# The samples' cross-attention in a decoder step: DRAM round trips and a two-slot ring against column tiles and a four-slot ring

## What is computed

```python
def _cross_attend(h, mk, mv, w_cq, w_co):
    b, t, _ = h.shape
    q = (h @ w_cq).reshape(b, t, CROSS_HEADS, CROSS_HEAD_DIM) * CROSS_HEAD_DIM ** -0.5
    s = jnp.einsum('bthe,bmhe->bhtm', q, mk).astype(jnp.float32)
    p = jax.nn.softmax(s, axis=-1).astype(mv.dtype)
    o = jnp.einsum('bhtm,bmhe->bthe', p, mv).reshape(b, t, D_MODEL)
    return o @ w_co
```

## Time and profile before

| | |
|---|---|
| median of 3 runs | 4460.27 us |
| profiled execution, its span | 4467.6 us |
| TensorE busy (matmuls) | 3948.9 us, 88% |
| VectorE busy | 1918.9 us, 43% |
| ScalarE busy | 1238.4 us, 28% |
| prompt's cross-attention, first score matmul to last copy | 2447.97 to 2518.2 us |
| samples' cross-attention, first VectorE instruction to the first of "co" on ScalarE | 2518.71 to 2682.23 us |

### The profile page before, as it was taken

The page is one execution under the profiler, slowest core; times in us unless marked ns, Lnnn a source line. Parts: engine busy times, 40 slices in busy tenths (PEclk is TensorE's granted clock), DMA queues, the critical chain, the costliest instruction groups (busy, mean ns, idle before and its releaser), DMA issues. The chain is left out here.

```text
span 4467.6 us, 73766 instructions
## 1 busy us (share of the span) xinstructions
PE 3948.9 (88%) x30029; PEld 3593.7 (80%) x30029; DVE 1918.9 (43%) x2612; ACT 1238.4 (28%) x1462; POOL 77.4 (2%) x120
## 2 busy tenths in 40 slices
PE   8989986757629998888998879999999999999998
PEld 8989975532228886778998419999999999999997
DVE  3224347758685555433232113333434334343343
ACT  3111126647613333422131202221211212122122
POOL 0000000000000000000000000000000000000000
PEclk9999988879858888999999989999999999999999
DMA  4322237759500000472222352222222222222222
GB/s 151 114 104 85 94 131 245 246 186 375 198 38 1 0 0 15 158 259 99 84 76 103 113 191 94 75 86 95 86 95 95 86 95 86 95 90 91 93 88 77
DMA packets 104474, 501.85 MB, mean 112 GB/s; under 512 B 14305, under 2 KB 20898, under 8 KB 67650
## 3 DMA queue, kind: packets, MB, share of 16 engines
q1 hardware_dynamic: 98082, 479.16, 30.1%
q0 software_dynamic: 6208, 19.93, 1.2%
HBM read 474.55 MB, written 24.50 MB: 112 GB/s over the span
## 5 line engine op out<-in xcount | busy, mean ns | idle before, releaser
L2112 PE MATMUL ps<-hf_hi,whi_f 128*128 128x260 f32 x2816 | 568.3, 283 | 19.1 <-DVE x L2102 11.1
L2112 PE MATMUL ps<-hf_hi,wlo_f 128*128 128x260 f32 x2816 | 567.9, 283 | 0.0
L2112 PE MATMUL ps<-hf_lo,whi_f 128*128 128x260 f32 x2816 | 567.0, 283 | 0.0
L182 ACT ACTIVATE whi_f<-raw 128x2048 fp32r<-128x2048 f32 x132 | 252.8, 1915 | 969.9 <-PE ps L2112 947.6
L2112 PEld LDWEIGHTS ps<-hf_hi,whi_f 128*128 128x128 f32 x2816 | 434.8, 189 | 20.9 <-DVE x L2102 14.5
L2112 PEld LDWEIGHTS ps<-hf_hi,wlo_f 128*128 128x128 f32 x2816 | 434.6, 189 | 0.0
L2112 PEld LDWEIGHTS ps<-hf_lo,whi_f 128*128 128x128 f32 x2816 | 433.6, 188 | 0.0
L186 DVE TENSOR_TENSOR wlo_f<-raw,whi_f 128x2048 fp32r<-128x2048 f32 x132 | 302.6, 2293 | 146.7 <-ACT whi_f L182 146.7
L220 PE MATMUL ps<-h_hi,whi_a 128*128 128x260 f32 x1600 | 324.2, 284 | 29.0 <-DVE h_lo L265 17.7
L220 PE MATMUL ps<-h_hi,wlo_a 128*128 128x260 f32 x1600 | 324.0, 284 | 0.0
L220 PE MATMUL ps<-h_lo,whi_a 128*128 128x260 f32 x1600 | 323.7, 284 | 0.0
(11 more groups left out here) (373 smaller groups left out, 6734.7 us busy)
## 6 DMA issues: line engine op xcount, KB each, us to landing
raw<-w SPq DMA_DIRECT2D x262, 1024.0 KB, 4.8
page_ring<-kc SPq DMA_DIRECT2D x128, 512.0 KB, 4.5
page_ring<-vc SPq DMA_DIRECT2D x64, 512.0 KB, 5.4
page_ring_more<-vc SPq DMA_DIRECT2D x64, 512.0 KB, 5.6
mem_ring<-mkc SPq DMA_DIRECT2D x8, 2048.0 KB, 8.0
mem_ring<-mvc SPq DMA_DIRECT2D x8, 2048.0 KB, 8.1
qkv<-ev_a POOLq DMA_DIRECT2D x24, 260.0 KB, 2.3
qkv_head<-qkv SPq DMA_DIRECT2D x8, 780.0 KB, 6.5
```

The lines of the kernel that those rows point to most:

```text
L182: act.activation(whi[:, u, :], raw[:, u, :], ACT.Copy).then_inc(whi_done, 1)
L2112: mm = pe.matmul(ps[:, 2 * u + s, 0:m], wt[:, wslot, kcol:kcol + 128], t[:, k, a:a + m], start=(first and wt is whi and t is th), stop=(la ...
```

## The change

Everything is in the samples' part, save that the ring is allocated before the prompt's cross-attention and its first four loads are issued in that block, behind the loads of `mk` and `mv`. In words:

- `ring` has four slots of 16 KB per partition. The 16 loads (8 of keys, 8 of values) are numbered through. Loads 0 to 3 are issued in the prompt's block without a wait; load n waits until n - 3 samples' products are done.
- The samples' part is one block. The queries of all samples are laid out once in `qz` (VectorE), so that 8 stationary columns go with a (sample, k-tile) and only the sample's own is not zero. `wz` is the same for the weights.
- The matmuls of head h write PSUM partitions 32h to 32h + 7, the four heads one after the other for each e, all samples into bank 0 (scores) or bank 1 (values). A matmul with zeros over the whole bank opens the accumulation of each; every other matmul adds.
- A one-column matmul over the full array follows the last product of each pass and releases the waiting engine.
- The softmax runs on the PSUM tile of 128 partitions itself. `xsrow`, `xorow`, `cur`, `rows` and the DMAs on them are gone, and so are ScalarE's and VectorE's copies per sample.

The diff, without what it deletes (all of L1817 to L1973 above):

```diff
+        MSLOTS = 4
+        crossing = ExitStack()
+        ring = sb(crossing, "mem_ring", [128, MSLOTS, KT * MEM])
...
+        def load_memory(sp, n):
+            if n >= MSLOTS:
+                sp.wait_ge(mem_c_used, n - MSLOTS + 1)
+            sp.dma_start(ring[:, n % MSLOTS, :], (mkc, mvc)[n // NS][n % NS, :, :, :].rearrange("p a b -> p (a b)"))\
+              .then_inc(mem_c_in[n % MSLOTS], 16)
...
                     sp.dma_start(mvb[:, :, :], mv_o.rearrange("m p n -> p m n")).then_inc(mkv_in, 16)
+                    for n in range(MSLOTS):
+                        load_memory(sp, n)
...
+            qz = sb(st, "x_q_columns", [128, 8 * 129])
+            wz = sb(st, "x_w_columns", [128, 560])
+            zero = sb(st, "x_zero", [128, 512])
...
                 @block.sync
                 def _(sp):
+                    for n in range(MSLOTS, 2 * NS):
+                        load_memory(sp, n)
 
                 @block.tensor
                 def _(pe):
+                    pe.wait_ge(S.sem, S.at("q"))
+                    for bank_ in range(2):
+                        pe.matmul(ps[:, bank_, :], zero[:, 0:128], zero[:, :], start=True, stop=False, skip_group_check=True)
+                    for b in range(NS):
+                        pe.wait_ge(mem_c_in[b % MSLOTS], 16 * (b // MSLOTS + 1))
+                        for e in range(4):
+                            for h in range(XH):
+                                k = 4 * h + e
+                                mm = pe.matmul(ps[32 * h:32 * h + NS, 0, 0:MEM], qz[:, b * 128 + k * NS:b * 128 + k * NS + NS],
+                                               ring[:, b % MSLOTS, k * MEM:(k + 1) * MEM], start=False, stop=False, skip_group_check=True)
+                        mm.then_inc(mem_c_used, 1)
+                    mm = pe.matmul(ps[:, 2, 0:1], zero[:, 0:128], zero[:, 0:1], start=True, stop=True)
+                    mm.then_inc(scores_done, 1)
                     pe.wait_ge(S.sem, S.at("scale"))
                     for m in range(2):
+                        mm = pe.matmul(ps[:, 4, m * 128:m * 128 + 128], sc[:, m * 128:m * 128 + 128], scale_[:, :], start=True, stop=True)
+                    mm.then_inc(weights_done, 1)
+                    pe.wait_ge(S.sem, S.at("w1"))
+                    for b in range(NS):
+                        n = NS + b
+                        pe.wait_ge(mem_c_in[n % MSLOTS], 16 * (n // MSLOTS + 1))
+                        for m in range(2):
+                            for h in range(XH):
+                                at = b * 64 + m * 32 + h * NS
+                                mm = pe.matmul(ps[32 * h:32 * h + NS, 1, :], wz[:, at:at + NS],
+                                               ring[:, n % MSLOTS, m * D + h * XD:m * D + h * XD + XD], start=False, stop=False,
+                                               skip_group_check=True)
+                        mm.then_inc(mem_c_used, 1)
+                    mm = pe.matmul(ps[:, 2, 0:1], zero[:, 0:128], zero[:, 0:1], start=True, stop=True)
+                    mm.then_inc(rows_done, 1)
+                    pe.wait_ge(S.sem, S.at("rows"))
+                    for e in range(4):
+                        mm = pe.transpose(ps[:, 5, e * 128:e * 128 + 128], oT[:, e * 128:e * 128 + 128], C("ident"))
+                    mm.then_inc(back_done, 1)
 
                 @block.scalar
                 def _(act):
                     act.wait_ge(S.sem, S.at("nm"))
+                    act.activation(sc[:, :], ps[:, 0, 0:MEM], ACT.Exp, bias=nm, scale=XS, accum_out=part).then_inc(exp_done, 1)
 
                 @block.vector
                 def _(dve):
                     def did(ins, name):
                         ins.then_inc(S.sem, 1)
                         dve.wait_ge(S.sem, S.at(name))
+                    did(dve.memset(qz[:, :], 0.0), "qz")
+                    did(dve.memset(wz[:, :], 0.0), "wz")
+                    did(dve.memset(zero[:, :], 0.0), "zero")
+                    did(dve.tensor_copy(qz[:, :].rearrange("p (b r) -> p b r", r=129)[:, :, 0:128:NS],
+                                        qc[:, :, SEQ:TOK].rearrange("p k b -> p b k")), "q")
+                    dve.wait_ge(scores_done, 1)
+                    did(dve.reduce_max(m1, ps[:, 0, 0:MEM], AX.X), "m1")
...
+                    did(dve.tensor_scalar(scale_[:, :], C("ident"), inv, None, ALU.mult), "scale")
+                    dve.wait_ge(weights_done, 1)
+                    for m in range(2):
...
+                        did(dve.tensor_copy(to, source), f"w{m}")
+                    dve.wait_ge(rows_done, 1)
+                    did(dve.tensor_copy(oT[:, :], ps[:, 1, :]), "rows")
+                    dve.wait_ge(back_done, 1)
                     for e in range(4):
+                        did(dve.tensor_copy(qc[:, e::4, SEQ:TOK],
+                                            ps[:, 5, e * 128:e * 128 + 128].rearrange("p (h x) -> p h x", h=XH)[:, :, 0:NS]), f"o{e}")
```

More of the change, by code:

```diff
@@ L1731, in decoder_kernel @@
         XS = XD ** -0.5
+        MSLOTS = 4
+        crossing = ExitStack()
+        ring = sb(crossing, "mem_ring", [128, MSLOTS, KT * MEM])
+        mem_c_in = [sem(f"mem_c_in{i}") for i in range(MSLOTS)]
+        mem_c_used = sem("mem_c_used")
+        def load_memory(sp, n):
[3 more added lines that the diff above has]
+              .then_inc(mem_c_in[n % MSLOTS], 16)
         with ExitStack() as st:
@@ L1816, in decoder_kernel @@
         with ExitStack() as st:
[L1817 to L1822, removed]
-            m1, nm, part, inv = [col[:, i:i + 1] for i in range(4)]
-            scale_ = sb(st, "x_scale", [NS * XH, NS * XH])
@@ L1825, in decoder_kernel @@
[L1825 to L1908, removed]
@@ L1909, in decoder_kernel @@
-            S = Steps(sem("xs_soft"), ["m1", "nm", "exp", "inv", "scale", "mm", "ws"])
+            qz = sb(st, "x_q_columns", [128, 8 * 129])
+            wz = sb(st, "x_w_columns", [128, 560])
+            zero = sb(st, "x_zero", [128, 512])
+            sc = sb(st, "x_scores", [128, MEM])
+            col = sb(st, "x_softmax_cols", [128, 4])
+            m1, nm, part, inv = [col[:, i:i + 1] for i in range(4)]
+            scale_ = sb(st, "x_scale", [128, 128])
+            oT = sb(st, "x_out_rows", [128, XD])
@@ L1910, in decoder_kernel @@
+            S = Steps(sem("xs_dve"), ["qz", "wz", "zero", "q", "m1", "nm", "inv", "scale", "w0", "w1", "rows"] + [f"o{e}" for e in range(4)])
+            scores_done, exp_done, weights_done, rows_done, back_done = [
+                sem(f"xs_{y}") for y in ("scores", "exp", "weights", "rows", "back")]
             with nc.Block() as block:
@@ L1924, in _ @@
                     act.wait_ge(S.sem, S.at("nm"))
-                    act.activation(sc[:, :], sc[:, :], ACT.Exp, bias=nm, scale=XS, accum_out=part).then_inc(S.sem, 1)
+                    act.activation(sc[:, :], ps[:, 0, 0:MEM], ACT.Exp, bias=nm, scale=XS, accum_out=part).then_inc(exp_done, 1)
                 @block.vector
@@ L1934, in _ @@
+                    dve.wait_ge(scores_done, 1)
+                    did(dve.reduce_max(m1, ps[:, 0, 0:MEM], AX.X), "m1")
                     did(dve.tensor_scalar(nm, m1, -XS, None, ALU.mult), "nm")
[L1935 removed]
+                    dve.wait_ge(exp_done, 1)
                     did(dve.reciprocal(inv, part), "inv")
[L1937 to L1938 removed]
@@ L1939, in _ @@
[L1939 to L1949, removed]
@@ L1952, in decoder_kernel @@
-            memory_pass(mvc, NS, value_operands, value_product,
-                        lambda u: ps[0:XH, 4 * u:4 * u + 4, :].rearrange("p a b -> p (a b)"),
-                        lambda b: xorow[bass.ds(b, 1), 0:XH * D].rearrange("o (h n) -> (o h) n", n=D), lambda u: rows[:, u, :])
-            own = xorow.rearrange("b (h m) -> (b h) m", m=D + XD)[:, 0:XD]
-            with nc.Block() as block:
-                @block.sync
-                def _(sp):
-                    sp.dma_start(oT[:, :], own).then_inc(rows_in, 16)
-                @block.tensor
-                def _(pe):
-                    pe.wait_ge(rows_in, 32)
-                    for e in range(4):
-                        mm = pe.transpose(ps[:, 4, e * 32:e * 32 + 32], oT[:, e * 128:e * 128 + 128], C("ident")[0:32, 0:32])
-                    mm.then_inc(q_ready, 1)
-                @block.vector
-                def _(dve):
-                    dve.wait_ge(q_ready, XH + 2)
-                    for e in range(4):
-                        dve.tensor_copy(qc[:, e::4, SEQ:TOK].rearrange("p h b -> p b h"),
-                                        ps[:, 4, e * 32:e * 32 + 32].rearrange("p (b h) -> p b h", h=XH)).then_inc(q_ready, 1)
@@ new lines, in _ @@
+                    did(dve.tensor_scalar(scale_[:, :], C("ident"), inv, None, ALU.mult), "scale")
+                    dve.wait_ge(weights_done, 1)
+                    for m in range(2):
+                        to = wz[:, m * 32:m * 32 + 8 * 65].rearrange("p (b r) -> p b r", r=65)[:, :, 0:32:NS]
```

(9 more changed lines are left out.)

5 lines of the change are left out of this document (removed).

## The result

The changed kernel takes 4376.87 us (median of four runs, 4374.3 to 4383.01), the kernel before 4458.69 (median of four) on the same chips: a ratio of 0.9818, 95% interval 0.9804 to 0.9832, or 81.8 us less. The forecast was 4375, the range 4364 to 4403.

What follows compares the result with a forecast made beforehand. The two-slot load cycle, 7.65 us per sample with no resource full, was taken to bound the samples' part. The rebuilt timeline's terms put "co" at 2596.8 instead of 2682.23: 4460.3 - 85.4 = 4375 us, range 4364 to 4403.

Steps and rivals of the forecast that it cites:

- The likeliest case: Samples' part: loads bound by DMA, four strips side by side, 85.4 us less, kernel 4375 us; chance 0.66.
- part: The samples' stretch, from VectorE's first clear to the start of "co" on ScalarE; 163.5 us before, 85.4 less forecast.
- Rate of the loads: Samples' stream: DMA rate decides with up to four loads outstanding; 5.3 us per load, bounds 4.9 and 5.75.
- Rival 1: Samples' stream: transfers fall to a shared memory's rate, 5.9 us per load, 6.6 more, kernel 4382 us; chance 0.10.
- The clock at the start: Opening matmuls with zeros: 1.7 us at full clock since TensorE idles 3 us only; 3.4 at the lower clock.
- Strips side by side: Samples' products: four heads' matmuls run at once, 1.75 us per sample; bounds 1.75 and 3.5, 6.99 if none.
- rival 3: Samples' products: strips don't work side by side, 6.99 us per sample, TensorE bounds, kernel 4421 us; chance 0.08.
- rival 4: Samples' products: every change of strip drains the array, 21 us slower than before, kernel 4482 us; chance 0.04.
- Cover of the softmax: Between samples 7 and 8: softmax takes 4.5 us while loads are under way, so it costs 0.
- Early loads: First four loads, in the prompt's block: land before the samples' part, cost 0; bounds 0 and 21 us.
- rival 5: Prompt's block: the early loads hold up `mv` by up to 21 us, kernel 4396 us; chance 0.04.
- Rival 2: Samples' stream: the deeper queue brings nothing, loads land every 7.65 us as now, kernel 4401 us; chance 0.07.

Runs made afterwards that it cites:

- Experiment 5: The changed kernel with all four heads' matmuls writing one strip, PSUM partitions 0 to 7 (result not the reference's): 4426.2 us.
- Experiment 2: The changed kernel with a ring of two slots instead of four, so only two early loads: 4403.5 us.
- experiment 3: The changed kernel without early loads: all 16 loads issued in the samples' own block, four slots kept: 4390.5 us.
- experiment 1: The changed kernel with the order of a sample's matmuls turned over, all of one head before the next: 4378.2 us.
- experiment 7: The changed kernel with the ring of the kernel before (two slots, no early loads), four strips kept: 4406.4 us.

## Why the prediction was right, and where its terms were off

The likeliest case came about: a stream bound by DMA, the four strips side by side. Its terms against the profile, counted from VectorE's first clear:

| term | forecast | measured |
|---|---|---|
| layout of the queries | 2.6 | 2.7 |
| matmuls with zeros | 1.7 | 3.7 |
| first products, to the issue of load 4 | 1.8 | 2.8 |
| that load, to the next burst | 7.8 | 7.95 |
| 11 more loads | 58.3 (5.3 each) | 54.6 (4.96 each) |
| last products | 2.6 | 1.8 |
| from there to "co" | 3.3 | 3.4 |
| part | 78.1 | 76.9 |

- **Rate of the loads.** 5.3 us was taken between 4.9 and 5.75; the lower bound was the right one. It came from the row with two ring loads in flight, 426 GB/s. The page loads' 378 GB/s pulled the estimate up, and that is an average over stretches of unequal rate (261 GB/s from 1065 to 1070 us). A shorter window inside the same 50 us, of the kernel before, shows that those loads too pass 400 GB/s:

```profile
1070.00:1080.00 10.00, 8.42 (x32) 2.40 (x32) 9.13 (x9) 7.96 (x9) 0.00 (x0) 1.00 1.02 413
```

Rival 1 is out: the bursts come 4.9 us apart. The Trainium skill (HBM Reference, Specifications) has one figure for a core that streams alone and one for a shared memory; 4.93 us and 5.86 are the estimates worked out from them. The profile agrees with the first: 4.9 us per load, and 431 GB/s.

- **The clock at the start.** "It idles 3 us only, so I take 1.7" failed. TensorE had waited 3.84 us, and the granted clock was 0.50, the lower level, over the whole of the zeros (2516.7 to 2520.4): they took 3.7 us, the bound kept for the range and 0.3 more. The first products paid too (0.71 up to 2523.2, then 1.00). 3 us late at the start and 4 us gained by the rate nearly cancel; that the part fits to 1.2 us is in part luck.
- **Strips side by side.** 1.75 us was forecast at full clock, a quarter of the 6.99 of one strip, though the earlier trace rows showed only two side by side. Measured are 1.91 for a burst by itself, the last pass's tail included, and 1.70 in the run of the first four samples ((7.87 - 2.76) / 3). That excludes rivals 3 and 4, and leaves no room for extra time per change of strip. Experiment 5 shows that the strips are the cause: without them a sample takes 7.0 us.
- **Cover of the softmax.** 3.7 us (forecast 4.5), and the bursts around it are two loads, 9.8 us, apart. Experiment 2 shows what it costs with less cover: 14.6 us for a pair of samples instead of some 12.
- **Early loads.** Worth 13 us (experiment 3, 2.4 of them the clock at its end), and `mv` is held up by 0.4 at most: rival 5 is out. Rival 2 is out too: with two slots it is still 6.1 us per sample, with four 4.9.
- **From part to kernel.** The part came out 1.2 us better than forecast, the kernel 1.9 worse; the difference lies outside the part, in the profiled execution that the sum was made against. The saving was 81.8 us, 3.6 less than the 85.4 forecast; the time is off by 1.9 only because the kernel before, too, came out 1.6 us below the median that the forecast started from. That is luck as well, and within the scatter of the medians.

## What to carry to other kernels

A ring costs per item the larger of three: the bytes at full rate, the products, and (latency plus products) divided by the number of slots. The runs fit it: one strip with the deep ring 7.0 us (products), one strip with the shallow one 7.4 to 7.6 (half of 7.9 + 7.0 + 0.3 is 7.6), four strips with the shallow one 5.9 to 6.2 (half of 7.9 + 3.6 + 0.4 is 5.95), four strips with the deep one 4.9 (bytes). The latency to take is that of a load with little else in flight, 7.9 us; in the changed kernel, with up to four in flight, the median from issue to landing is 16.0, and a load spends part of that behind the ones before it. Work out all three from one profile before deepening the ring or shortening the products, since either alone may only uncover the next: here 11.5 and 29.9 us alone, 59.9 together. And when a stage ends up with one resource full and another idle, look at the stage beside it for the reverse; weaving the two brought 47 us on top of the 82 of the change.

## What the runs showed that was not expected

- TensorE doesn't need alternating strips in the program: four passes of one strip in a row before the next still ran four strips at once (1.93 us for 16 passes of 512 columns at full clock); with eight in a row 32 passes of 256 took 4.51 us by themselves and 3.5 per sample back to back, where four strips at once take 1.91 and 1.70, and one strip 7.0. How far ahead TensorE looks was not measured beyond these two orders.
- The granted clock was 0.60 from 2531 to 2548 us of the changed kernel, where bursts of 1.9 to 3.6 us were parted by waits of 1.1 to 3.3 us, and 1.00 in the same window of experiment 1, where TensorE was busy for 15.67 of 17 us. The lower level costs nothing while the products are hidden behind the loads. A burst takes up to 3.6 instead of 1.9 us, and this shows in the time, where they are not hidden: in the slot's cycle of experiments 2 and 7 and at the end of 3.
- Three to four loads of 2 MB in flight kept all DMA engines busy at 431 GB/s for 17 us.
